# Feed-forward blocks as seven products of 2x2 blocks in an fp32 decoder step

## What is computed

```python
def _swiglu(x, w_gate, w_up, w_down):
    return (jax.nn.silu(x @ w_gate) * (x @ w_up)) @ w_down

def _layer(x, ...):
    x = _layer_norm(ALPHA * x + 0.5 * _swiglu(x, ffn1...), ln1_g, ln1_b)
    ...   # h = x @ w_in; pooling, window attention, cross attention; merged
    x = _layer_norm(ALPHA * x + merged @ w_o, ln2_g, ln2_b)
    x = _layer_norm(ALPHA * x + 0.5 * _swiglu(x, ffn2...), ln3_g, ln3_b)
```

## Time and profile before

| | us |
|---|---|
| median of 3 runs | 2711.49 |
| lowest, highest | 2710.77, 2712.06 |
| span of the profiled execution | 2709.7 |
| PE busy in it | 2605.9 (96%) |
| DVE busy | 1028.6 (38%) |
| ACT busy | 794.3 (29%) |
| POOL busy | 123.3 (5%) |

### The profile page before, as it was taken

How to read it: one execution, slowest core, us unless ns; L and a number is a source line. 1 busy time by engine, 2 the same in 40 slices (tenths; PEclk the granted TensorE clock), 3 DMA queues, 4 the chain that set the end, 5 groups by cost and what they waited for, 6 DMA issues and landing times.

```text
span 2709.7 us, 47591 instructions
## 1 busy us (share of the span) xinstructions
PE 2605.9 (96%) x19010; PEld 2554.8 (94%) x19010; DVE 1028.6 (38%) x1410; ACT 794.3 (29%) x1273; POOL 123.3 (5%) x164
## 2 busy tenths in 40 slices
PE   6999999899999899999989999989999998999995
PEld 6999999899999899999989999989999998999994
DVE  3323323645444632323342333254453454223224
ACT  3222211424422422221242222142442223222213
POOL 1000000220000200000010000011100002000001
PEclk8999999989999999999999999999999999999998
DMA  5222222322122122222212222232112222222221
GB/s 205 85 88 79 83 88 91 111 71 60 56 78 80 60 78 85 77 85 93 82 61 84 87 78 86 93 111 94 47 53 79 77 70 64 83 85 78 86 93 66
DMA packets 72128, 224.30 MB, mean 83 GB/s; under 512 B 17601, under 2 KB 20545, under 8 KB 71233
## 3 DMA queue, kind: packets, MB, share of 16 engines
q1 hardware_dynamic: 72032, 222.99, 24.9%
HBM read 218.89 MB, written 6.04 MB: 83 GB/s over the span
## 4 chain that ended last, share of the span: by engine, by line
issue 66%; PE 29%; POOL 2%; DVE 1%; ACT 1%; DMA 1%; POOLq 1%; DVEq 0%; ACTq 0%; SPq 0%
PE pair L959 9%; PE pair L963 9%; PE pair L961 9%; POOL xl L889 1%; DVE wl L601 1%; POOL x L895 0%; POOL tmp L912 0%; ACT wh L408 0%; PE S L1100 0%; POOLq L913 0%; DMA par<-in_par 0%; DMA cst<-in_cst 0%; POOL tmp L938 0%; POOL tmp L947 0%; DVEq L684 0%
## 5 line engine op out<-in xcount | busy, mean ns | idle before, releaser
L959 PE MATMUL pair<-xh,wh 128*128 128x288 f32 x3904 | 876.0, 302 | 37.5 <-DVE xl L694 22.8
L961 PE MATMUL pair<-xl,wh 128*128 128x288 f32 x3904 | 862.7, 299 | 0.0
L963 PE MATMUL pair<-xh,wl 128*128 128x288 f32 x3904 | 862.7, 299 | 0.0
L601 DVE TENSOR_TENSOR wl<-raw,wh 128x1024 fp32r<-128x1024 f32 x382 | 471.1, 1233 | 990.6 <-ACT wh L408 982.6
L408 ACT ACTIVATE wh<-raw 128x1024 fp32r<-128x1024 f32 x382 | 404.1, 1058 | 1371.5 <-PE pair L963 1292.7
L959 PEld LDWEIGHTS pair<-xh,wh 128*128 128x128 f32 x3904 | 645.1, 192 | 55.5 <-DVE xl L694 26.2
L961 PEld LDWEIGHTS pair<-xl,wh 128*128 128x128 f32 x3904 | 646.1, 192 | 0.0
L963 PEld LDWEIGHTS pair<-xh,wl 128*128 128x128 f32 x3904 | 645.2, 192 | 0.0
L959 PE MATMUL pair<-Hh,wh 128*128 128x288 f32 x1408 | 310.1, 295 | 0.0
L963 PE MATMUL pair<-Hh,wl 128*128 128x288 f32 x1408 | 310.0, 294 | 0.0
L961 PE MATMUL pair<-Hl,wh 128*128 128x288 f32 x1408 | 308.4, 293 | 0.0
(11 more groups left out here) (166 smaller groups left out, 1798.8 us busy)
## 6 DMA issues: line engine op xcount, KB each, us to landing
raw<-in_wblk SPq DMA_DIRECT2D x382, 512.0 KB, 3.3
mcs<-in_mks SPq DMA_DIRECT2D x2, 2048.0 KB, 10.4
mcs<-in_mvs SPq DMA_DIRECT2D x2, 2048.0 KB, 9.7
x<-in_x SPq DMA_DIRECT2D x1, 2304.0 KB, 10.8
out_y<-x SPq DMA_DIRECT2D x2, 1152.0 KB, 5.3
cst<-in_cst SPq DMA_DIRECT2D x1, 1105.0 KB, 5.7
mem<-in_mem SPq DMA_DIRECT2D x2, 512.0 KB, 5.1
kcs<-in_kcs SPq DMA_DIRECT2D x2, 512.0 KB, 3.6
```

Source lines behind the costliest of these rows:

```text
L601: nc.vector.tensor_tensor(wl[:, s, :], raw[:, s, :], wh[:, s, :].bitcast(F32), ALU.subtract).then_inc(w_lo, 1)
L959: nc.tensor.matmul(out(h), wt[0], xt[0](h), start=(kk == 0), stop=False)
L961: nc.tensor.matmul(out(h), wt[0], xt[1](h), start=False, stop=False)
L963: last = nc.tensor.matmul(out(h), wt[1], xt[0](h), start=False, stop=(kk == nk - 1))
```

## The change

The feed-forward products are made by a scheme of seven products in place of eight. A weight block of 2x2 tiles (rows 2i and 2i+1 of the contraction; gate and up column tile, or two output tiles) times the 2x2 blocks of x (two channel tiles, two halves of the columns) is put together from P1 to P7, each the product of one form of the weights and one form of x. P1, P2 and P4 take plain weight quarters, P5, P6, P7 and P3 take sums of quarters s1 to s4.

Work runs in 38 units per block: a G unit (gate and up of one hidden tile, 4 pairs of contraction tiles, quarters of 128x512) and a D unit (two output tiles, two or three pairs of hidden tiles, 128x256 or 128x384), in the order of `SEQ`. There are 22 G and 16 D units; D results are added onto x after each part of the contraction. Per unit:
- SP loads four quarters in one transfer (1 MB for a G unit), two buffers rawA and rawB.
- POOL makes the four sums (`prepare`) and subtracts the low parts of the four rounded sums (`rest_of_sum`).
- ACT rounds all seven forms (`fill`), copies the partial sums p1, u2, u3 out of PSUM and applies silu. Each product has one slot for its rounded weights, refilled when the product of the unit before is done.
- DVE subtracts the low parts of the three plain quarters, adds banks to the copies (c12, c22, c11), makes the hidden halves `hf`, and after each odd hidden tile four sums of them and the low parts of all seven forms (864 and 1152 columns).
- TensorE runs P1, then P4 and P3 of the unit before, then P6, P5, P7, P2. P6 waits for the copy of P1, P7 for the copy after P6, P3 for c22.

x also needs its sum forms, made by POOL (`forms`, tile tf), rounded by ACT, low parts by DVE. The hidden layer is kept for three tile pairs only. The loops are unrolled, and many buffers share addresses. The mixing stage is as before but for its buffers; the layer norm ahead of the mixing stage no longer overlaps the last block. In the core of the diff, `-` is the old loop on TensorE:

```diff
-                with pe.Fori(1, FC) as j:
-                    for s in range(2):
-                        project(l, pq(l, Q_GU[f]) + j, s, n_use(l, U_GU[f]) + j)
...
+PARTS = [(0, 1), (2, 3, 4), (5, 6, 7), (8, 9, 10)]
+SEQ = []
+for _p, _last in enumerate((4, 10, 16, 21)):
+    SEQ += [("G", _j) for _j in range((0, 5, 11, 17)[_p], _last + 1)]
+    SEQ += [("D", _p, _d) for _d in range(4)]
...
+SUM = {"P5": 0, "P6": 1, "P7": 2, "P3": 3}
...
+            def fill(fb, u, prod):
...
+                if u > 0:
+                    act.wait_ge(f_done, done(fb, u - 1, prod))
...
+                if prod in SUM:
+                    act.wait_ge(f_sum, (fb * FU + u) * 4 + SUM[prod] + 1)
+                    src = sums[:, SUM[prod], 0:n]
+                else:
+                    act.wait_ge(fraw_in[u % 2], (fb * (FU // 2) + u // 2 + 1) * 16)
+                    src = quarter(u, prod, n)
+                nc.scalar.activation(slot((hiA, hiB), prod, n), src, ACT.Copy).then_inc(f_hi, 1)
...
+                    if g:
+                        act.wait_ge(f_done, done(fb, u, "P1"))
+                        act.wait_ge(ep_free, unit_count(fb, u - 1))
+                        nc.scalar.activation(p1[:, :], al[u % 2], ACT.Copy).then_inc(al_act, 1)
+                    fill_next("P1")
+                    fill_rest()
+                    silu_before()
+                    if g:
+                        act.wait_ge(f_done, done(fb, u, "P6"))
+                        act.wait_ge(de_free, unit_count(fb, u - 1))
+                        nc.scalar.activation(u2[:, :], al[u % 2], ACT.Copy).then_inc(al_act, 1)
+                    fill_next("P6")
+                    round_hidden(0)
+                    fill_next("P5")
+                    if g:
+                        act.wait_ge(f_done, done(fb, u, "P7"))
+                        act.wait_ge(de_read, unit_count(fb, u - 1))
+                        nc.scalar.activation(u3[:, :], al[u % 2], ACT.Copy).then_inc(al_act, 1)
+                    round_hidden(1)
+                    fill_next("P7")
+                    if g:
+                        act.wait_ge(ep_free, unit_count(fb, u))
+                        nc.scalar.activation(c11[:, :], c11[:, :], ACT.Silu).then_inc(c11_silu, 1)
+                    fill_next("P2")
+            def layer_norm(l, n):
...
+            def rest_of_quarter(fb, u, prod):
+                n = pairs_of(SEQ[u]) * P
+                dve.wait_ge(f_hi, filled(fb, u, prod))
+                nc.vector.tensor_tensor(slot((loA, loB), prod, n), quarter(u, prod, n),
+                                        slot((hiA, hiB), prod, n).bitcast(F32), ALU.subtract).then_inc(f_lo_p, 1)
...
+                    def finish_before():
+                        if g_old:
+                            dve.wait_ge(f_done, done(fb, u - 1, "P4"))
+                            dve.wait_ge(c11_silu, g_count(fb, u - 1))
+                            nc.vector.scalar_tensor_tensor(out=hf[:, odd, :], in0=c11[:, :], scalar=0.5, in1=al[r_old],
+                                                           op0=ALU.mult, op1=ALU.mult).then_inc(al_free, 1)
+                            dve.wait_ge(f_done, done(fb, u - 1, "P3"))
+                            nc.vector.tensor_tensor(c12[:, :], u2[:, :], de[r_old], ALU.add).then_inc(de_free, 1)
...
+                    def hidden_second():
+                        if g_old:
+                            dve.wait_ge(c12_silu, g_count(fb, u - 1))
+                            last = nc.vector.scalar_tensor_tensor(out=hf[:, 2 if odd else 7, :], in0=c12[:, :], scalar=0.5,
+                                                                  in1=c22[:, :], op0=ALU.mult, op1=ALU.mult)
...
+                    def hidden_sums():
+                        if odd:
+                            dve.drain()
+                            nc.vector.tensor_tensor(hf[:, 3, :], hf[:, 7, :], hf[:, 0, :], ALU.subtract)
+                            nc.vector.tensor_tensor(hf[:, 4, :], hf[:, 2, :], hf[:, 7, :], ALU.subtract)
+                            dve.drain()
+                            nc.vector.tensor_tensor(hf[:, 5, :], hf[:, 2, :], hf[:, 3, :], ALU.subtract)
+                            dve.drain()
+                            nc.vector.tensor_tensor(hf[:, 6, :], hf[:, 1, :], hf[:, 5, :], ALU.subtract).then_inc(h_sums, 1)
+                    def rest_of_hidden(group):
+                        if odd:
+                            n = SEQ[u - 1][1] // 2
+                            forms = slice(3 * group, 3 + 4 * group)
+                            dve.wait_ge(h_hi, h_count(fb, n, group))
+                            nc.vector.tensor_tensor(htl[:, n % 3, forms, :], hf[:, forms, :],
+                                                    hth[:, n % 3, forms, :].bitcast(F32), ALU.subtract).then_inc(h_lo, 1)
...
+                            nc.vector.tensor_tensor(c22[:, :], u3[:, :], de[r], ALU.add).then_inc(de_read, 1)
...
+                        p1_of_down()
+                        finish_before()
+                        if u < FU:
+                            rest_of_quarter(fb, u, "P4")
+                            rest_of_next("P1")
+                        hidden_second()
+                        p6_of_down()
+                        hidden_sums()
+                        rest_of_hidden(0)
+                        p5_and_p7()
+                        rest_of_hidden(1)
+                    if g:
+                        dve.wait_ge(f_done, done(fb, u, "P2"))
+                        dve.wait_ge(al_act, g_count(fb, u) * 3 - 2)
...
+                a11, a12, a21, a22 = (fraw[u % 2][:, i * n:(i + 1) * n] for i in range(4))
+                s1, s2, s3, s4 = (sums[:, i, 0:n] for i in range(4))
+                pool.wait_ge(fraw_in[u % 2], (fb * (FU // 2) + u // 2 + 1) * 16)
+                pool.drain()
+                nc.gpsimd.tensor_tensor(s1, a21, a22, ALU.add).then_inc(f_sum, 1)
+                pool.drain()
+                nc.gpsimd.tensor_tensor(s2, s1, a11, ALU.subtract).then_inc(f_sum, 1)
+                nc.gpsimd.tensor_tensor(s3, a11, a21, ALU.subtract).then_inc(f_sum, 1)
+                pool.drain()
+                nc.gpsimd.tensor_tensor(s4, a12, s2, ALU.subtract).then_inc(f_sum, 1)
+                for prod in ("P6", "P5", "P7"):
+                    rest_of_sum(fb, u, prod)
...
+                    nc.gpsimd.tensor_tensor(t1, b12, b11, ALU.subtract)
+                    nc.gpsimd.tensor_tensor(t3, b22, b12, ALU.subtract)
+                    pool.drain()
+                    nc.gpsimd.tensor_tensor(t2, b22, t1, ALU.subtract)
+                    pool.drain()
+                    nc.gpsimd.tensor_tensor(t4, b21, t2, ALU.subtract)
+                    pool.drain().then_inc(xf_sums, 1)
...
+                for u in range(1, FU):
+                    rest_of_sum(fb, u - 1, "P3")
+                    prepare(fb, u)
+                rest_of_sum(fb, FU - 1, "P3")
...
+                if prod in SUM:
+                    pe.wait_ge(f_lo, lo_count(fb, u, prod))
+                else:
+                    pe.wait_ge(f_lo_p, lo_p_count(fb, u, prod))
...
+                elif prod == "P6":
+                    pe.wait_ge(read, count - 2)
+                elif prod == "P7":
+                    pe.wait_ge(read, count - 1)
+                elif prod == "P4":
+                    pe.wait_ge(read, count)
+                elif prod == "P5":
+                    pe.wait_ge(de_free, unit_count(fb, u - 2))
+                elif prod == "P3":
+                    pe.wait_ge(de_read, unit_count(fb, u))
+                else:
+                    pe.wait_ge(ep_free, unit_count(fb, u - 2))
...
+                    cols = slice(i * P, (i + 1) * P)
+                    wt_hi = slot((hiA, hiB), prod, n * P)[:, cols]
+                    wt_lo = slot((loA, loB), prod, n * P)[:, cols]
+                    start = i == 0 and prod in ("P1", "P5", "P2")
+                    nc.tensor.matmul(bank, wt_hi, xt[0], start=start, stop=False, skip_group_check=True)
+                    nc.tensor.matmul(bank, wt_hi, xt[1], start=False, stop=False, skip_group_check=True)
+                    last = nc.tensor.matmul(bank, wt_lo, xt[0], start=False, stop=i == n - 1, skip_group_check=True)
+                last.then_inc(f_done, 1)
...
+                for u in range(1, FU):
+                    if u != TAIL:
+                        product(fb, u, "P1")
+                    product(fb, u - 1, "P4")
+                    product(fb, u - 1, "P3")
+                    if u == TAIL:
+                        product(fb, u, "P1")
+                    for prod in ("P6", "P5", "P7", "P2"):
+                        product(fb, u, prod)
```

887 lines of the change are left out of this document (585 added, 302 removed).

## The result

The changed kernel takes 2980.05 us (median; runs 2975.04 to 2989.44), the kernel before 2711.77 us beside it: 1.099 times as long, 95% interval 1.097 to 1.101. The profiled execution has a span of 2976.4 us, 266.7 us more than before.

What follows compares the result with a forecast made beforehand. The prediction took the number of TensorE matmuls to bound the feed-forward blocks before the change. To 2709.7 us it added 133 for four blocks, 63 outside them and 1.8 from span to median: 2907 us, range 2700 to 3060.

Steps and rivals of the forecast that it cites:

- Turns: POOL and DVE operations with two SBUF operands alternate; a 512-column DVE operation costs POOL 0.44 us, a 1152-column one 1.13.
- Gate unit, 14.0 us: Pace of a G unit in the feed-forward blocks, taken as the middle of two bounds, 13.3 and 14.85 us.
- stream bound: G unit limited by POOL's own operations: 10.4 us plus 2.9 us mean delay from DVE, 13.3 us.
- chain bound: G unit limited by DVE's queue, each such operation waiting for a whole POOL operation: 29.7 us a pair, 14.85 a unit.
- The chain's first leg: Behind an odd hidden tile, DVE's work from the end of P3 to c22: 13.9 us, where 5 would do undisturbed.
- Down units: D units of three pairs between 9.2 and 9.6 us, taken 9.4; of two pairs 6.8 us.
- The down units of the last part: D units with four more two-operand sums for the mean: 10.0 to 14.4 us, taken 11.0.
- Between the blocks: Outside the blocks: +18 us at each of three block starts, +3 at each of two mixing stages, +3 start; +63 us.
- The signs: Expected evidence: POOL busy 85% or more in a block, TensorE waiting for c22 and POOL's low part, G units 13 to 15 us.
- B: Rival: turns hardly matter in the blocks and TensorE stays the bound, G units at 11.2 us; 2546 us, chance 0.13.
- C: Rival: POOL runs at its fast price of 1.0 us an operation, 12.5 us a G unit; 2717 us, chance 0.10.
- D: Rival: waits through DVE bind throughout, or TensorE's clock falls after gaps, +123 us; 3030 us, chance 0.15.

Runs made afterwards that it cites:

- run 2: Changed kernel, but from the second block on VectorE's operations with two SBUF operands take the second from an unused bank (values wrong); 2754.9 us.
- Run 4: Changed kernel with VectorE's add for c22 moved ahead of the hidden sums and the first low part of the hidden forms; 3043.1 us.
- run 6: Changed kernel with ScalarE's copy of P1 issued ahead of the roundings of the form sums at three block starts; 2975.6 us.
- Run 3: Changed kernel with POOL's sums and low parts cut to 16 columns from the third unit of the later three blocks (values wrong); 2718.6 us.
- run 7: Changed kernel with weight sums' low parts on VectorE, early copy of P1, and POOL's first three sums no longer waiting for P3's low part; 2823.0 us.
- run 10: Changed kernel with weight sums' low parts on VectorE, early copy of P1, new VectorE order, and early POOL sums only inside gate parts; 2728.6 us.

## Why the prediction was right, step by step

The forecast was 2907 us, 7% slower, range 2700 to 3060; measured 2980 us. The side, the mechanism and the bound were right; one wait in the block had no term, and the terms outside the blocks were too small.

**Turns.** Right, and shown by run 2. A POOL low part of 512 columns takes 1.58 instead of 1.29 us, a low part of 864 columns on VectorE 1.93 instead of 1.05 us (run 2 gives the undisturbed value), one of 1152 columns 1.93 instead of 1.35: 0.9 and 0.6 us more, where I said about 1. That operations which read a bank are free of turns was right too: 454 ns at 288 columns, beside a busy POOL.

**Gate unit, 14.0 us, between a stream bound of 13.3 and a chain bound of 14.85.** Measured 56.0 / 4 = 14.0 in the second block. Over the whole first block it is 14.3: a stretch of 400.6 us, less 4 x 6.6 and 8 x 9.2 us of down units, over 21 intervals; without TensorE's waits ahead of the down parts, below, the block's 22 gate units take 307.4 us, 14.0 each. The chain's first leg, 13.9 us forecast from the end of P3 to c22, is 12.5 to 13.4 us in the gate units behind an odd tile. I had called the chain bound the step most likely to fail, since it takes each wait for a whole POOL operation; its first leg was 4 to 11% high. That the middle of the two bounds came out is in part luck, since no row picked it. Run 4 shows that the late operation can't be moved by itself.

**Down units.** 9.4 forecast, 9.2 measured (low parts of P3 at 257.01, 266.21 and 275.43 us), two pairs 6.6 instead of 6.8.

**The hand-over to the down units** is the step that had no term. The first of four down units waits for VectorE's low part of the last hidden pair, which follows the four stretched sums. In the first block TensorE waits for it four times, 1.89, 4.12, 4.11 and 6.83 us, 16.9 us together. The longest stands ahead of the last part:

```profile
484.88 0.61 PE L1538 MATMUL pair<-hth,hiA 128*128 128x288 f32 x1 [6.83 <-DVE htl L951]
```

From 473 to 498 us TensorE is busy for 16.6 of 25 us at a granted clock of 0.80.

**The down units of the last part** take 13.0 and 11.8 us (two of them, by POOL's low parts of P3), inside my bounds of 10.0 to 14.4, but I took a value near the lower end. From the end of the last gate unit's P3 (477.1 us) to the block's last matmul (530.85) there are 53.7 us; without the wait of 6.8 that is 46.9, forecast 44.

A block: gate units -0.6 us against the forecast, down units of the middle parts -2.2, those of the last part +2.9, the four hand-overs +16.9, together 471.4 instead of 454.4. That the first three cancel is luck. Against before, the forecast growth was 33.2 and the measured one 46.1 us; the difference is 12.9 and not 17.0 us, because the block of before is 425.3 us in the trace where the prediction reckoned 421.2. Four blocks: 52 of the 71 us by which the profiled span, 2976.4 us, exceeds the sum of 2905.7.

**Between the blocks.** Forecast +18 for each of three starts; measured 22.8 to 24.2 inside the block (its growth less the first block's), and one of them 4.9 ahead of it, 75 us and not 54. The mixing stage cost 12.9 us instead of 6, the start 7.4 instead of 3. That is 33 us missing. The four pairs of form sums at 4.4 us were about right (4.2 to 5.6 us apart in run 6). That P6 would be fed pair by pair was wrong: ScalarE's copy of P1 stands behind all four roundings and a table load, so P6 began only when the last was done. By run 6 this is worth only 1.0 to 1.7 us a block. The end, counted at nothing, gave 13.6 us back. 52 + 33 - 13.6 = 71 us.

**The signs.** The wait for c22 (line 964) ahead of P3: right, 63.3 us in 28 waits. POOL's low part ahead of P6: there is such a wait, but it is small: 6.2 us in 4 for TensorE's matmuls and 33.3 us in 17 for its weight loads, which run ahead of them. The larger one there is ScalarE's copy (p, 98.3 us, of which the three block starts are 53.6; u, 39.5 us), and ScalarE had been counted at nothing. Run 3, in which ScalarE's work is untouched and gate units have 11.1 to 11.2 us, shows that ScalarE's own work is not what binds. POOL busy 85% or more: 88% from 60 to 180 us, 83% from 180 to 480 us, 84% over both, so just missed.

**The rivals.** B (TensorE stays the bound) needed the turns to vanish; run 2 makes them vanish and has 11.5 us a unit. Its price was wrong too: 2546 us, where run 3 with TensorE as the bound in every block comes to an estimated 2642. C fell: POOL's operations of 512 columns have 1.29 us in run 2, those on one tile too, not 1.0. Of D, the clock's part is real but small: granted clock 0.50 behind a gap of 3 us, 0.97 on average from 60 to 480 us. Run 4 comes near D's price, 3043 us where I gave 3030, but not by D's signs: its units have 14.8 us and a granted clock of 0.93 in the middle of a block.

One thing stays open: why early sums lengthen a down part by 6 us in run 7. The waits that grow are those for the adds onto x; no run takes apart what delays them, and run 10 only shows that leaving the early sums out there avoids it.
